# Two decoder layers on one core: the small expert's gate and up turned by transposes instead of folding matmuls

## The chip, the core and the metric

The kernel runs on one core of a Trainium2 chip, in one launch. The metric is the device time of the program in microseconds. The work of a core is split over engines that run side by side and meet at semaphores: TensorE (PE, matmuls; its weight loads are listed as PEld), VectorE (DVE), ScalarE (ACT), GpSimd (POOL), and SyncE (SP), which here issues the weight transfers.

## The reference

Two decoder layers over 256 tokens of width 1024, all in float32. Layer 0 has two kinds of sparse attention and a dense SwiGLU, layer 1 a latent attention and a mixture of 8 experts, 2 for each token. The change touches only the mixture:

```
def swiglu(h, w_gate, w_up, w_down):
    return (jax.nn.silu(h @ w_gate) * (h @ w_up)) @ w_down

    logits = (ht @ w_router).astype(jnp.float32) + b_router.astype(jnp.float32)
    top_val, top_idx = lax.top_k(logits, TOP_K)
    gates = jax.nn.softmax(top_val, axis=-1)
    combine = jnp.sum(jax.nn.one_hot(top_idx, N_EXPERTS, dtype=jnp.float32) * gates[..., None], axis=1)
    for e in range(N_EXPERTS):
        y = y + combine[:, e:e + 1].astype(h.dtype) * swiglu(ht, w_gate[e], w_up[e], w_down[e])
```

w_gate and w_up of an expert are 1024 x 3584, w_down is 3584 x 1024.

## The kernel before

**Split weights.** Each factor of a matmul is split into a high part, rounded to the PE's fast float32r, and a low part that holds the rest. Weights come in chunks of 128 x 2048 (1 MB) into `raw`, a ring of 7 slots. For each chunk SyncE issues the transfer once TensorE has used the chunk 7 before it; ScalarE writes `w_hi` (ring of 6, L665 in the mixture); VectorE writes `w_lo` (L1298) as raw minus w_hi into the place of raw; TensorE multiplies. These three steps are called the split of a chunk below.

**Pairs.** Experts are sorted by their number of tokens. A large one (up to 128 tokens) and a small one (up to 64, HALF) are run as a pair p of 84 chunks k; there are four pairs, so 336 chunks. Gate and up weights of both come in turn: 8 chunks for the large (12 matmuls of 512 columns each), 8 for the small (8 matmuls each), up to chunk 47; then 4 and 4; then 14 down chunks of the large (56 to 69) and 14 of the small (70 to 83). The hidden width 3584 is cut into 7 units j of 512, and a unit's gate and up sums are ready after the chunks that `large_ups(j)` or `small_ups(j)` names.

**A large unit.** ScalarE writes silu(gate) into `sge` (L694), VectorE multiplies it with up into `he` (L1363), TensorE turns the 128 x 512 block by four transposes (L1941), ScalarE and VectorE write the high and the low half, `e_hi` (L698) and `e_lo` (L1368).

**A small unit.** The 64 tokens stand twice in the stationary operand, on 64 partitions with their high parts and on 64 with their low parts, so that two matmuls do the work of three; gate and up then lie in PSUM as two halves over the partitions, and these have to be added. ScalarE copies gate and up into `sge` and `he` (L721, L724). TensorE turns and adds in one step: 8 fp32 matmuls (L1948) with `fold`, two identities of 64 on top of each other, into one bank. ScalarE takes the silu of the turned gate into `sT` (L716), VectorE the product into `hT` (L1387), ScalarE the high half into `es` (L727), VectorE the low half (L1391).

**Order.** Each engine runs a loop over k written out by hand. ScalarE and VectorE run 4 chunks ahead (ELEAD). `units(k, done, late)` names the units whose step falls to chunk k: `done(u) + late + u % 2 == k`. A step that stands in a loop over k waits in its place: behind it on its engine stand all splits of later chunks. Also in these loops are the gather of the next pair's tokens (L1850, at `GATHER_AT`, chunk 60), the small expert's gather (L1859), the way back to the tokens (L1877, L1878, added by VectorE at L1347), TensorE's transpose of the gated pick (L1866, at `PICK_AT`, chunk 16), and VectorE's `back` (4 chunks later), `gated_picks` (5), `picks` (8) and `small_picks` (9).

## Time and profile before

| | us |
|---|---|
| median of 3 runs | 1442.11 |
| lowest and highest | 1435.95, 1446.27 |
| the profiled execution | 1440.49 |
| its span in the profile | 1438.5 |
| TensorE busy | 1346.6 (94%) |
| VectorE busy | 1144.9 (80%) |
| ScalarE busy | 974.8 (68%) |

The mixture's chunks begin at about 514 us and end at about 1428 us of the span. The mean granted clock of TensorE over the span is 0.981 of full speed. The profile gives for each engine its busy time and, for a row, the idle time in front of it and who ended that. Matmuls are pipelined, so their busy times overlap; the distance between two starts tells what one costs.

### The profile page before, as it was taken

To read this page: it belongs to the slowest core of one execution; us is meant where nothing else is said; L and a number is where in the kernel's file an instruction comes from. 1 tells how busy PE (TensorE), PEld (TensorE's weight loads), DVE (VectorE), ACT (ScalarE), POOL (GpSimd) and SP (SyncE) were. 2 spreads that over 40 slices of the span, in tenths; PEclk is the share of its full clock that TensorE was granted. 3 is DMA by queue.
4 is the path that set the end of the run, shared out by engine and by line. 5 is a ranking of instruction groups with operands and counts; after the bars stand their busy time and mean duration, and the time that the engine had idled before them with its cause. 6 is when DMAs were issued, how large, how long until landed. Compare 5 with 4: busy or idle time off the path is not lost.

```text
span 1438.5 us, 17054 instructions
## 1 busy us (share of the span) xinstructions
PE 1346.6 (94%) x6497; PEld 1099.1 (76%) x6498; DVE 1144.9 (80%) x1161; ACT 974.8 (68%) x969; POOL 39.2 (3%) x47
## 2 busy tenths in 40 slices
PE   6987999999779889999999999999999999999996
PEld 5765788878766778778877887878877887878884
DVE  4776464462675489999899999899999999999896
ACT  4475545342477447888777878777888867788874
POOL 1012000000004000000000000000000000000000
PEclk9999999999889899999999999999999999999999
DMA  8641455553440449999999999999999999999995
GB/s 311 220 138 59 146 186 165 185 184 108 135 133 1 146 165 405 389 379 402 347 410 376 383 387 396 358 402 363 397 399 381 364 387 391 394 391 389 401 381 207
DMA packets 134940, 423.02 MB, mean 294 GB/s; under 512 B 7888, under 2 KB 14790, under 8 KB 134854
## 3 DMA queue, kind: packets, MB, share of 16 engines
q1 hardware_dynamic: 133756, 419.10, 77.8%
q0 software_dynamic: 864, 2.68, 0.6%
q8 instruction: 54, 0.88, 0.2%
q14 instruction: 32, 0.26, 0.1%
q10 hardware_dynamic: 234, 0.09, 0.0%
HBM read 420.77 MB, written 1.07 MB: 293 GB/s over the span
## 4 chain that ended last, share of the span: by engine, by line
PE 65%; DVE 20%; ACT 6%; DMA 6%; issue 3%; ACTq 0%; DVEq 0%; SPq 0%
PE PS L1510 18%; PE PS L1512 17%; PE PS L1511 17%; DVE w_lo L1298 12%; DMA raw<-in_w_up_o_dram 3%; PE PS L1948 3%; ACT w_hi L665 2%; DMA raw<-in_w_down_o_dram 2%; DVE w_lo L795 2%; PE PS L1913 1%; PE PS L1914 1%; PE PS L1850 1%; ACT w_hi L365 1%; PE PS L1859 1%; DVE he L1363 1%
## 5 line engine op out<-in xcount | busy, mean ns | idle before, releaser
L1298 DVE TENSOR_TENSOR w_lo<-raw,w_hi 128x2048 fp32r<-128x2048 f32 x336 | 762.2, 2287 | 62.1 <-ACT w_hi L665 60.0
L665 ACT ACTIVATE w_hi<-raw 128x2048 fp32r<-128x2048 f32 x336 | 639.1, 1916 | 123.5 <-DMA raw<-in_w_down_o_dram 49.4
L1510 PE MATMUL PS<-w_hi,a_hi 128*128 128x512 f32 (+5 forms) x848 | 330.1, 389 | 25.7 <-DVE w_lo L1298 14.4
L1512 PE MATMUL PS<-w_hi,a_lo 128*128 128x512 f32 (+5 forms) x848 | 323.7, 382 | 0.0
L1511 PE MATMUL PS<-w_lo,a_hi 128*128 128x512 f32 (+5 forms) x848 | 323.2, 381 | 0.0
L1510 PEld LDWEIGHTS PS<-w_hi,a_hi 128*128 128x128 f32 x848 | 161.2, 190 | 64.1 <-issue 28.9
L1512 PEld LDWEIGHTS PS<-w_hi,a_lo 128*128 128x128 f32 x848 | 161.4, 190 | 30.6
L1511 PEld LDWEIGHTS PS<-w_lo,a_hi 128*128 128x128 f32 x848 | 161.5, 190 | 27.2
L1913 PE MATMUL PS<-w_hi,a_hi 128*128 128x512 f32 x448 | 179.6, 401 | 2.2 <-DVE w_lo L1298 1.6
L1914 PE MATMUL PS<-w_lo,a_hi 128*128 128x512 f32 x448 | 175.2, 391 | 0.0
L795 DVE TENSOR_TENSOR w_lo<-raw,w_hi 128x2048 fp32r<-128x2048 f32 (+4 forms) x70 | 139.4, 2018 | 39.4 <-ACT w_hi L365 39.2
L365 ACT ACTIVATE w_hi<-raw 128x2048 fp32r<-128x2048 f32 (+4 forms) x70 | 115.4, 1698 | 12.6 <-PE PS L1512 12.6
L1913 PEld LDWEIGHTS PS<-w_hi,a_hi 128*128 128x128 f32 x448 | 84.1, 188 | 25.4 <-DVE w_lo L1298 9.2
L1914 PEld LDWEIGHTS PS<-w_lo,a_hi 128*128 128x128 f32 x448 | 84.2, 188 | 16.3
L1913 PE MATMUL PS<-w_hi,es 128*128 128x512 f32 x224 | 90.1, 402 | 5.0 <-DVE w_lo L1298 4.8
L1510 PE MATMUL PS<-w_hi,e_hi 128*128 128x512 f32 x224 | 88.9, 397 | 1.9 <-DVE w_lo L1298 1.9
L1914 PE MATMUL PS<-w_lo,es 128*128 128x512 f32 x224 | 88.3, 394 | 0.0
L1512 PE MATMUL PS<-w_hi,e_lo 128*128 128x512 f32 x224 | 88.1, 393 | 0.0
L1511 PE MATMUL PS<-w_lo,e_hi 128*128 128x512 f32 x224 | 87.8, 392 | 0.0
L1913 PEld LDWEIGHTS PS<-w_hi,es 128*128 128x128 f32 x224 | 42.1, 188 | 20.7 <-DVE w_lo L1298 6.3
L1510 PEld LDWEIGHTS PS<-w_hi,e_hi 128*128 128x128 f32 x224 | 42.1, 188 | 14.3 <-issue 4.5
L576 ACT ACTIVATE sg<-PS,nst 128x512 f32<-128x512 f32 (+1 forms) x12 | 7.2, 650 | 64.6 <-PE PS L1512 64.6
(287 smaller groups left out, 1413.5 us busy)
## 6 DMA issues: line engine op xcount, KB each, us to landing
raw<-in_w_gate_o_dram SPq DMA_DIRECT2D x112, 1024.0 KB, 9.3
raw<-in_w_up_o_dram SPq DMA_DIRECT2D x112, 1024.0 KB, 10.0
raw<-in_w_down_o_dram SPq DMA_DIRECT2D x112, 1024.0 KB, 8.0
raw<-in_w_in_e_dram SPq DMA_DIRECT2D x12, 1024.0 KB, 7.6
raw<-in_w_down_e_dram SPq DMA_DIRECT2D x11, 1024.0 KB, 4.9
raw<-in_w_gate_e_dram SPq DMA_DIRECT2D x10, 1024.0 KB, 5.1
raw<-in_w_up_e_dram SPq DMA_DIRECT2D x10, 1024.0 KB, 5.1
raw<-in_w_out_e_dram SPq DMA_DIRECT2D x4, 1024.0 KB, 5.0
```

Source lines behind the costliest of these rows:

```text
L365: nc.scalar.activation(w_hi[:, c % STG, 0:n], raw[:, c % RAW, 0:n], ACT.Copy).then_inc(hi_done, 1)
L665: nc.scalar.activation(w_hi[:, c % STG, :], raw[:, c % RAW, :], ACT.Copy).then_inc(hi_done, 1)
L795: nc.vector.tensor_tensor(w_lo[:, c % RAW, 0:n], raw[:, c % RAW, 0:n], w_hi[:, c % STG, 0:n], ALU.subtract).then_inc(lo_done, 1)
L1298: nc.vector.tensor_tensor(w_lo[:, c % RAW, :], raw[:, c % RAW, :], w_hi[:, c % STG, :], ALU.subtract).then_inc(lo_done, 1)
L1363: nc.vector.tensor_tensor(he[:, j % 2, :], PS[:, up_bank(j), :], sge[:, j % 2, :], ALU.mult)\
L1510: nc.tensor.matmul(dst, xh, wh, start=first, stop=False)
L1511: nc.tensor.matmul(dst, xh, wl, start=False, stop=False)
L1512: return nc.tensor.matmul(dst, xl, wh, start=False, stop=last)
L1850: ins = nc.tensor.matmul(PS[:, 4 + h, d * P:(d + 1) * P], xn[:, t, dc * P:(dc + 1) * P], pick[:, t, :], start=t == 0, stop=t == 1)
L1913: nc.tensor.matmul(dst, xs, wh, start=first, stop=False)
L1914: return nc.tensor.matmul(dst, xs, wl, start=False, stop=last)
L1948: ins = nc.tensor.matmul(PS[:, small_turn_bank(j), at:at + HALF], halves[:, j % 2, f * P:(f + 1) * P], fold[:, :], start=True, stop=True)
```

## The change

The 8 fp32 matmuls of a small unit's turn become 8 plain transposes. The two halves are then not added by TensorE: gate fills one whole bank and up the next, each as 4 blocks of 64 high and 64 low columns. ScalarE copies the low columns of both banks (512 elements per partition) into a new buffer `gh`; VectorE adds the high columns from PSUM to it in place; ScalarE takes the silu of the gate part in place; VectorE multiplies in place; high and low halves follow as before, each one chunk later. `SMALL_TURN` gives the first bank of a unit's two, out of the pairs 6/7, 4/5 and 2/3. To make banks 4 and 5 free, what used them there moves: transpose of the pick, back and the picks by 8 chunks, the gather by 4. `sT`, `hT` and `fold` go.

```diff
-PICK_AT, GATHER_AT = 16, DOWN_L + 4
+PICK_AT, TURN_AT, GATHER_AT = 16, 24, DOWN_L + 8
-        sT, z = place(z, "sT", [P, 2, 4 * HALF])
-        hT, z = place(z, "hT", [P, 2, 4 * HALF])
+        gh, z = place(z, "gh", [P, 2, 2, 4 * HALF])
-            return 6 + u % 2 if u < FE_TILES - 1 else 7
+        SMALL_TURN = (6, 4, 6, 4, 6, 2, 4)
...
@@ ScalarE @@
                     for j in units(k, small_ups, 5):
                         act.wait_ge(sem("sm_tr"), j + 1 + p * FE_TILES)
                         if j >= 2:
-                            act.wait_ge(sem("sm_mul"), j - 1 + p * FE_TILES)
-                        nc.scalar.activation(sT[:, j % 2, :], PS[:, small_turn_bank(j), 0:4 * HALF], ACT.Silu)\
-                            .then_inc(sem("sm_silu"), 1)
+                            act.wait_ge(sem("sm_lo"), j - 1 + p * FE_TILES)
+                        b = SMALL_TURN[j]
+                        nc.scalar.activation(gh[:, j % 2, :, :].rearrange("p u (f t) -> p u f t", f=4),
+                                             PS[:, b:b + 2, :].rearrange("p u (f h t) -> p u f h t", f=4, h=2)[:, :, :, 1, :],
+                                             ACT.Copy).then_inc(sem("sm_low"), 1)
+                    for j in units(k, small_ups, 6):
+                        act.wait_ge(sem("sm_sum"), j + 1 + p * FE_TILES)
+                        nc.scalar.activation(gh[:, j % 2, 0, :], gh[:, j % 2, 0, :], ACT.Silu).then_inc(sem("sm_silu"), 1)
...
-                    for j in units(k, small_ups, 7):
+                    for j in units(k, small_ups, 8):
                         act.wait_ge(sem("sm_mul"), j + 1 + p * FE_TILES)
                         nc.scalar.activation(es[:, 4 * j:4 * j + 4, 0:HALF],
-                                             hT[:, j % 2, :].rearrange("p (f t) -> p f t", f=4), ACT.Copy)\
+                                             gh[:, j % 2, 1, :].rearrange("p (f t) -> p f t", f=4), ACT.Copy)\
...
@@ VectorE @@
-                    for j in units(k, small_ups, 6):
+                    for j in units(k, small_ups, 5):
+                        b = SMALL_TURN[j]
+                        both = gh[:, j % 2, :, :].rearrange("p u (f t) -> p u f t", f=4)
+                        dve.wait_ge(sem("sm_low"), j + 1 + p * FE_TILES)
+                        nc.vector.tensor_tensor(both, PS[:, b:b + 2, :].rearrange("p u (f h t) -> p u f h t", f=4, h=2)[:, :, :, 0, :],
+                                                both, ALU.add).then_inc(sem("sm_sum"), 1)
+                    for j in units(k, small_ups, 7):
                         dve.wait_ge(sem("sm_silu"), j + 1 + p * FE_TILES)
-                        if j >= 2:
-                            dve.wait_ge(sem("sm_lo"), j - 1 + p * FE_TILES)
-                        nc.vector.tensor_tensor(hT[:, j % 2, :], PS[:, small_turn_bank(j), 4 * HALF:8 * HALF], sT[:, j % 2, :],
-                                                ALU.mult).then_inc(sem("sm_mul"), 1)
-                    for j in units(k, small_ups, 8):
+                        nc.vector.tensor_tensor(gh[:, j % 2, 1, :], gh[:, j % 2, 1, :], gh[:, j % 2, 0, :], ALU.mult)\
+                            .then_inc(sem("sm_mul"), 1)
+                    for j in units(k, small_ups, 9):
...
-                    if k == PICK_AT + 4:
+                    if k == TURN_AT + 4:
                         back(2 * p)
...
@@ TensorE @@
             def turn_small(j):
                 for u, halves in enumerate((sge, he)):
                     for f in range(4):
-                        at = (4 * u + f) * HALF
-                        ins = nc.tensor.matmul(PS[:, small_turn_bank(j), at:at + HALF], halves[:, j % 2, f * P:(f + 1) * P],
-                                               fold[:, :], start=True, stop=True)
+                        ins = nc.tensor.transpose(PS[:, SMALL_TURN[j] + u, f * P:(f + 1) * P], halves[:, j % 2, f * P:(f + 1) * P],
+                                                  ident)
...
-                    if k == PICK_AT:
-                        pe.wait_ge(sem("moe_add"), 8 * p + 4)
+                    if k == TURN_AT:
+                        pe.wait_ge(sem("sm_sum"), 2 + p * FE_TILES)
                         turn_pick(2 * p)
...
                     for j in units(k, small_ups, 2):
                         pe.wait_ge(sem("sm_ev"), j + 1 + p * FE_TILES)
-                        if j == FE_TILES - 1:
-                            pe.wait_ge(sem("sm_mul"), j + p * FE_TILES)
-                        else:
-                            pe.wait_ge(sem("moe_alo"), j + 1 + p * FE_TILES)
+                        if SMALL_TURN[j] == 6:
+                            pe.wait_ge(sem("moe_alo"), j + 2 + p * FE_TILES)
+                        if j == 1:
+                            pe.wait_ge(sem("moe_add"), 8 * p + 4)
+                        if j == 3:
+                            pe.wait_ge(sem("moe_back"), 2 * p + 1)
+                        if j == 5:
+                            pe.wait_ge(sem("sm_eg"), 6 + p * FE_TILES)
                         turn_small(j)
                     if follow and k == GATHER_AT:
+                        pe.wait_ge(sem("sm_sum"), FE_TILES + p * FE_TILES)
                         gather(p + 1)
```

On VectorE, in the first pair from chunk 16 on, there stands in a row before (`L1298` is the w_lo of a chunk, `x4` four chunks in a row):

```order
L1298 TENSOR_TENSOR w_lo<-raw,w_hi 128x2048 x4
L1352 TENSOR_REDUCE st<-PS 128x1
L1353 TENSOR_SCALAR backT<-PS 128x256
L1298 TENSOR_TENSOR w_lo<-raw,w_hi 128x2048
L1318 TENSOR_SCALAR pickg<-cst,pos,comb 128x128 x2
L1298 TENSOR_TENSOR w_lo<-raw,w_hi 128x2048
L1387 TENSOR_TENSOR hT<-PS,sT 128x256
L1298 TENSOR_TENSOR w_lo<-raw,w_hi 128x2048
L1387 TENSOR_TENSOR hT<-PS,sT 128x256
L1298 TENSOR_TENSOR w_lo<-raw,w_hi 128x2048
L1391 TENSOR_TENSOR es<-hT,es 128x4x64
L1304 TENSOR_SCALAR pick<-cst,pos 128x128 x2
```

And after the change, at the same place (w_lo is now L1299, the sum L1388, the product L1392, the large unit's he L1364):

```order
L1299 TENSOR_TENSOR w_lo<-raw,w_hi 128x2048 x5
L1388 TENSOR_TENSOR gh<-PS,gh 128x512
L1299 TENSOR_TENSOR w_lo<-raw,w_hi 128x2048
L1388 TENSOR_TENSOR gh<-PS,gh 128x512
L1299 TENSOR_TENSOR w_lo<-raw,w_hi 128x2048
L1392 TENSOR_TENSOR gh<-gh 128x256
L1299 TENSOR_TENSOR w_lo<-raw,w_hi 128x2048
L1392 TENSOR_TENSOR gh<-gh 128x256
L1299 TENSOR_TENSOR w_lo<-raw,w_hi 128x2048
L1396 TENSOR_TENSOR es<-gh,es 128x4x64
L1299 TENSOR_TENSOR w_lo<-raw,w_hi 128x2048
L1364 TENSOR_TENSOR he<-PS,sge 128x512
```

The back and the picks have left the place, the first sum stands one chunk ahead of where the first product stood, and the product and the halves follow one chunk later.

On ScalarE, around units 2 and 3 of the first pair, there stands before (L665 is the w_hi of a chunk, L694 the large unit's silu):

```order
L665 ACTIVATE w_hi<-raw 128x2048 x3
L716 ACTIVATE sT<-PS 128x256
L665 ACTIVATE w_hi<-raw 128x2048
L694 ACTIVATE sge<-PS 128x512
L716 ACTIVATE sT<-PS 128x256
L665 ACTIVATE w_hi<-raw 128x2048
L694 ACTIVATE sge<-PS 128x512
L727 ACTIVATE es<-hT 128x4x64
L665 ACTIVATE w_hi<-raw 128x2048
L727 ACTIVATE es<-hT 128x4x64
```

And after (w_hi is L662, the large silu L691, the copy of the low half L714, the silu L719, the high half L729):

```order
L662 ACTIVATE w_hi<-raw 128x2048 x3
L714 ACTIVATE gh<-PS 128x512
L662 ACTIVATE w_hi<-raw 128x2048
L691 ACTIVATE sge<-PS 128x512
L714 ACTIVATE gh<-PS 128x512
L719 ACTIVATE gh<-gh 128x256
L662 ACTIVATE w_hi<-raw 128x2048
L691 ACTIVATE sge<-PS 128x512
L719 ACTIVATE gh<-gh 128x256
L662 ACTIVATE w_hi<-raw 128x2048
L729 ACTIVATE es<-gh 128x4x64
```

The copy stands where sT stood, a silu for each unit has come in behind it, and the high half is one chunk later.

## Rows read from the trace of the kernel before

**Rows 1.** Windows: busy us (x rows) by engine, then clock, DMA share, GB/s.
```profile
796.30:839.10 42.80, 41.82 (x203) 33.99 (x202) 40.40 (x33) 34.59 (x28) 0.00 (x0) 1.00 1.00 387
839.10:881.30 42.20, 41.43 (x204) 34.21 (x202) 39.37 (x25) 35.56 (x28) 0.00 (x0) 1.00 1.01 381
...
796.30:1025.80 229.50, 222.85 (x1068) 182.08 (x1066) 212.71 (x138) 180.00 (x132) 0.00 (x0) 1.00 0.99 383
```

**Rows 2.** Waits from 500 to 1438 us: us in total, times, longest.
```profile
DVE w_lo L1298 <- ACT w_hi L665: 60.0, 100, 2.2
...
ACT sT L716 <- PE PS L1948: 18.0, 18, 1.8
...
ACT es L727 <- DVE hT L1387: 8.4, 8, 1.2
```

**Rows 3.** The chain of waits, 858 to 883 us: start, us on the chain.
```profile
858.23 2.20 DVE w_lo L1298
860.43 0.60 DVE he L1363
...
870.51 2.21 DVE w_lo L1298
872.86 0.47 PE PS L1510
881.29 1.75 PE PS L1948 x16
```

**Rows 4.** Timeline of PE at a large and a small unit's turn: start, us.
```profile
818.83 0.60 PE L1941 MATMUL PS<-cst,he 128*128 128x128 f32 x4
...
819.50 0.39 PE L1914 MATMUL PS<-w_lo,a_hi 128*128 128x512 f32 x1
...
843.52 1.00 PE L1948 MATMUL PS<-cst,sge 128*128 128x64 f32 x8
...
845.54 0.39 PE L1511 MATMUL PS<-w_lo,a_hi 128*128 128x512 f32 x1
```

**Rows 5.** Timeline of ACT around units 2, 3 and 4, idle before in brackets.
```profile
836.73 1.92 ACT L665 ACTIVATE w_hi<-raw 128x2048 fp32r<-128x2048 f32 x1 [0.64 <-DMA raw<-in_w_up_o_dram]
839.29 1.91 ACT L665 ACTIVATE w_hi<-raw 128x2048 fp32r<-128x2048 f32 x1 [0.64 <-DMA raw<-in_w_up_o_dram]
...
845.45 0.39 ACT L716 ACTIVATE sT<-PS 128x256 f32<-128x256 f32 x1 [1.13 <-PE PS L1948]
...
883.12 0.60 ACT L694 ACTIVATE sge<-PS 128x512 f32<-128x512 f32 x1 [2.00 <-PE PS L1948]
```

**Rows 6.** Timeline of DVE around units 2 and 3.
```profile
843.81 2.29 DVE L1298 TENSOR_TENSOR w_lo<-raw,w_hi 128x2048 fp32r<-128x2048 f32 x1 [0.28 <-ACT w_hi L665]
846.02 0.42 DVE L1387 TENSOR_TENSOR hT<-PS,sT 128x256 f32<-128x256 f32 x1
847.67 2.29 DVE L1298 TENSOR_TENSOR w_lo<-raw,w_hi 128x2048 fp32r<-128x2048 f32 x1 [1.24 <-ACT w_hi L665]
```

**Rows 7.** Groups by line and shape, 400 to 1438 us: busy us, mean ns.
```profile
L1363 DVE TENSOR_TENSOR he<-PS,sge 128x512 f32<-128x512 f32 x28 | 19.2, 684 | 0.0
...
L724 ACT ACTIVATE he<-PS 128x512 f32<-128x512 f32 x28 | 16.3, 582 | 0.2 <-PE PS L1914 0.2
...
L1391 DVE TENSOR_TENSOR es<-hT,es 128x256 fp32r<-128x256 f32 x28 | 11.7, 419 | 0.0
L1387 DVE TENSOR_TENSOR hT<-PS,sT 128x256 f32<-128x256 f32 x28 | 11.7, 417 | 0.0
L727 ACT ACTIVATE es<-hT 128x256 fp32r<-128x256 f32 x28 | 11.7, 417 | 9.2 <-DVE hT L1387 8.4
...
L716 ACT ACTIVATE sT<-PS 128x256 f32<-128x256 f32 x28 | 10.7, 382 | 18.1 <-PE PS L1948 18.0
```

**Rows 8.** Timeline of PE just after the mixture's first long wait.
```profile
516.91 0.63 PE L1511 MATMUL PS<-w_lo,a_hi 128*128 128x512 f32 x1
517.34 0.63 PE L1512 MATMUL PS<-w_hi,a_lo 128*128 128x512 f32 x1
```

More of the change, by code:

```diff
@@ L212, in hybrid_trunk @@
         backT, z = place(z, "backT", [P, S], f32r)
-        fold = cst[:, K_MASK:K_MASK + HALF]
         PS = ctx.enter_context(nc.psum_tensor("PS", [P, 8, NT], f32))
@@ L256, in small_up_bank @@
             return u % 2 if u < FE_TILES - 1 else 1
-        def small_turn_bank(u):
-            return 6 + u % 2 if u < FE_TILES - 1 else 7
+        SMALL_TURN = (6, 4, 6, 4, 6, 2, 4)
         def pair_chunk(k):
@@ L1279, in by_size @@
                 step(ins)
-                step(nc.vector.tensor_tensor(fold[:, :], ident[:, 0:HALF], ident[:, HALF:P], ALU.add))
             def combine():
@@ L1390, in pair @@
+                    for j in units(k, small_ups, 7):
+                        dve.wait_ge(sem("sm_silu"), j + 1 + p * FE_TILES)
+                        nc.vector.tensor_tensor(gh[:, j % 2, 1, :], gh[:, j % 2, 1, :], gh[:, j % 2, 0, :], ALU.mult)\
+                            .then_inc(sem("sm_mul"), 1)
+                    for j in units(k, small_ups, 9):
                         dve.wait_ge(sem("sm_hi"), j + 1 + p * FE_TILES)
                         nc.vector.tensor_tensor(es[:, 4 * j:4 * j + 4, HALF:P],
-                                                hT[:, j % 2, :].rearrange("p (f t) -> p f t", f=4),
+                                                gh[:, j % 2, 1, :].rearrange("p (f t) -> p f t", f=4),
@@ L1393, in pair @@
                                                 es[:, 4 * j:4 * j + 4, 0:HALF], ALU.subtract).then_inc(sem("sm_lo"), 1)
-                    if k == PICK_AT + 4:
+                    if k == TURN_AT + 4:
                         back(2 * p)
-                    if k == PICK_AT + 5:
+                    if k == TURN_AT + 5:
                         gated_picks(p + PAIRS, p + PAIRS, HALF)
-                    if follow and k == PICK_AT + 8:
+                    if follow and k == TURN_AT + 8:
                         picks(p + 1, P)
-                    if follow and k == PICK_AT + 9:
+                    if follow and k == TURN_AT + 9:
@@ L1968, in pair_waits @@
                     else:
-                        pe.wait_ge(sem("moe_back"), 2 * p + 1)
+                        pe.wait_ge(sem("sm_sum"), 4 + p * FE_TILES)
                 elif kl == DOWN:
@@ L1973, in pair_waits @@
                     else:
-                        pe.wait_ge(sem("sm_eg"), FE_TILES - 1 + units0)
+                        pe.wait_ge(sem("sm_sum"), FE_TILES - 1 + units0)
                 if kl >= DOWN and (kl - DOWN) % 2 == 0:
@@ L1995, in pair @@
                         if j >= 2:
-                            pe.wait_ge(sem("sm_mul"), j - 1 + p * FE_TILES)
+                            pe.wait_ge(sem("sm_sum"), 2 * (j // 2) - 1 + p * FE_TILES)
                         else:
@@ L2001, in pair @@
                         pe.wait_ge(sem("sm_ev"), j + 1 + p * FE_TILES)
-                        if j == FE_TILES - 1:
-                            pe.wait_ge(sem("sm_mul"), j + p * FE_TILES)
-                        else:
-                            pe.wait_ge(sem("moe_alo"), j + 1 + p * FE_TILES)
+                        if SMALL_TURN[j] == 6:
[6 more added lines that the diff above has]
+                            pe.wait_ge(sem("sm_eg"), 6 + p * FE_TILES)
                         turn_small(j)
                     if follow and k == GATHER_AT:
+                        pe.wait_ge(sem("sm_sum"), FE_TILES + p * FE_TILES)
                         gather(p + 1)
                     if k == DOWN_S + 3:
-                        pe.wait_ge(sem("sm_mul"), FE_TILES + p * FE_TILES)
+                        pe.wait_ge(sem("sm_sum"), FE_TILES + p * FE_TILES)
                         if follow:
```

## The prediction

> **What bounds the kernel now.** I read the windows first, then the waits, the chain and the timelines. Everything the change touches lies in the mixture of experts, four pairs of 84 chunks of 1 MB, some 229 us a pair. Over one pair TensorE is busy 222.9 of 229.5 us, VectorE 212.7, ScalarE 180.0, and the transfers show a share of 0.99 of their 16 engines [rows 1]. So three resources stand within 8% of each other: taking work from one of them hits the next soon. The reader should see in the waits that VectorE waits 60.0 us for ScalarE's w_hi, that ScalarE waits 18.0 us for the small expert's turn (L1948) at its sT, and that it waits 8.4 us in 8 places for VectorE's product [rows 2]. The chain shows where each engine sets the time: VectorE row by row in the small expert's chunks (858.23 to 870.51, with 0.60 us for each 512-wide row between two w_lo of 2.20 us), then TensorE from 872.86 through the large expert's chunks and the turn at 881.29 [rows 3]. TensorE thus paces the large phases, with the turns in them; VectorE and the transfers pace the small ones. In the steady stretch the splits of ScalarE start 2.56 us apart (836.73, 839.29) because transfers land so [rows 5]. 16 chunks at that pace are 41.0 us, and the window of 16 chunks takes 42.2 [rows 1]: no more than 1.2 us is to be had in such a group before the transfers are the bound. The group before it, read from turn to turn in the same way, takes 42.8, so 1.8.
>
> **The turn on TensorE.** A small unit's turn now runs from 843.52 to the point from which the next matmuls run at full pace: the second of them starts at 845.54, matmuls of 512 columns start 0.23 apart, so the turn costs 845.54 - 0.23 - 843.52 = 1.79 us for 16 passes (8 fp32 matmuls, two records each). The large unit's four transposes run from 818.83 in the same way to 819.50 - 0.23, which is 0.44 us; their 0.60 us of busy time with 0.27 for the last makes 0.11 us from one to the next [rows 4]. Eight transposes are then 0.44 + 4 x 0.11 = 0.88 us, and a turn loses 0.91 us. 28 turns: 25.5 us of TensorE.
>
> **VectorE.** Before, a unit has a product of 256 (L1387, PSUM source, 417 ns) and a low half of 256 (L1391, 419 ns). After, it has a sum of 512 with one PSUM operand, the shape of L1363 (684 ns busy, 0.60 in the chain), a product of 256 from SBUF like L1391, and the same low half [rows 3, 7]. Busy times overlap the next row by 0.08, so 256 elements cost 0.34 on the path. Added: 0.60 us a unit, 16.8 us in all. No row reads PSUM in runs of 64; I take the contiguous row's price, between nothing extra and twice it, and take the row because its element count and engines are the same. The Trainium skill, Perfetto Trace Analysis, in its tips on VectorE and ScalarE, puts an instruction's data access at some 60 ns from SBUF and 125 ns from PSUM for VectorE; by that the product from SBUF would be 65 ns cheaper, 1.8 us over 28 units. Rows L1387 and L1391 differ by 2 ns the other way, so the trace does not bear it out here.
>
> **ScalarE.** sT (382 ns from PSUM) becomes a copy of 512 out of PSUM, like L724 (582 ns), and a Silu of 256 from SBUF, like L727 (417 ns) [rows 7]: about 0.6 us a unit, 17 us in all, beside 180 of 229.5 us busy. It has room for it, except where someone waits for the split behind it.
>
> **What of this lies on the path, place by place.** I step through one pair.
> *Units 0 to 3 (two groups of 16 chunks).* At 845.45 ScalarE's sT of the second unit has waited 1.13 us for TensorE, the split behind it comes late, and VectorE, done with its row at 846.02, idles 1.24 us until 847.67 [rows 5, 6]. After the change both turns before that point are shorter, 1.8 us together, so the copy of the low half starts when ScalarE is free, and that stall goes. In its place come two sums, 1.20 us. The first falls into the slack that VectorE has while it runs at the transfers' 2.56 against its own 2.21 (0.35 us a chunk). Net for VectorE: -1.24 + 1.20 - 0.35, some -0.4 us. That is the floor. The ceiling is the transfers' pace, 1.2 to 1.8 us, 1.5 on average. It is approached because a slot of raw is refilled only when TensorE has used it: chunks finished up to 1.8 us sooner refill the ring sooner. I take the middle, 0.9 us a group, 1.8 a pair.
> *Units 4 and 5.* At 883.12 ScalarE's sge has waited 2.00 us for the turn at 881.29 [rows 3, 5], so the shorter turn counts directly, -0.91. From there to the split of the first down chunk VectorE sets the pace; that stretch had two products (0.68) and now has two sums and one product (1.54): +0.86. Net nothing (-1.2 to +0.5).
> *Unit 6.* Its turn lies among 14 large chunks in a row, where TensorE is the bound: -0.91, the sum beside it. At worst the following small chunks swallow it.
> *What only moves.* back, the gated picks and both picks (some 1.9 us a pair on VectorE) go 8 chunks later, TensorE's transpose of the pick from chunk 16 to 24, the gather from chunk 60 to 64. The first four leave the place where the two sums now stand, and land before the next large phase. Queued behind them are w_lo rows that TensorE reaches only later in that phase; without that cover they cost what they free at the old place. I cost both at nothing. The new waits on TensorE (for sums) name sums that VectorE issues before the w_lo that TensorE has already used, so they are met. ScalarE's Silu waits for a sum of the chunk before; behind it is queued the next split, and VectorE waits for that. The fold constant goes (one row). SP's and POOL's queues keep their order.
>
> Sum per pair: 1.8 + 0 + 0.9 = 2.7 us; four pairs 10.9 us. The profiled execution took 1440.5 us (span 1438.5), the median is 1442.1, so the first becomes 1429.6 and the second **1431**. Bounds of the unknowns: 0.4 x 2 - 0.5 + 0 = 0.3 us a pair gives 1441; 1.5 x 2 + 1.2 + 0.9 = 5.1 us a pair gives 1422. A change under 1%, 14.4 us, can hardly be told from none in this kernel.
>
> **Rivals.**
> *The sums eat it.* VectorE is 93% busy and takes 16.8 us more; if the refill of the ring gains nothing, only the floor is left: 1441. For it: 858.23 to 870.51 has no gap on VectorE [rows 3]. Against: TensorE's share is higher still. Chance 0.20.
> *More than forecast.* If TensorE's lag is what starves the transfers everywhere, also in the down chunks and after the gathers, 25.5 us of it come back nearly in full and each pair goes towards 84 x 2.56 = 215 us until VectorE's 217 bounds it. 5 to 6 us a pair: 1420. For it: 14.5 us a pair lie between 229.5 and 215. Against: VectorE would have to be 97% busy. Chance 0.20.
> *Slower, by the handshake.* A unit now passes between ScalarE and VectorE six times instead of four: low half, sum, Silu, product, high, low. The sum stands in the same chunk as the copy it needs. If the copy ends more than VectorE's 2.2 us after the split before it, VectorE stands still with all its w_lo behind it, and TensorE behind those. A wait of this kind (es for the product) costs 8.4 / 8 = 1.05 us [rows 2]. If every unit pays half of it beside its own sum, 28 x (0.5 + 0.6) = 31 us stand against what the places above save before their sums, 2 x (1.24 + 0.35) + 2 x 0.91 = 5.0 us a pair, 20 us: 1453. It decides where TensorE is over 1.6 us behind at the copy; sT waited 1.0 us on average (18 times), before turns got shorter. Chance 0.12.
> *It doesn't do what it says.* If an fp32 transpose took two passes like the fold, no turn would get shorter and the sums would remain: 16.8 us less the slack of 0.35 at 8 of them, so 1456. Rows L1941 show one record each, 0.11 apart [rows 4]. Chance 0.02.
> *The clock.* Around both kinds of turn the granted clock is 1.00, the upper level of 2.4 GHz [rows 1]; where it was low, after waits of TensorE, 512 columns start 0.43 apart instead of 0.23 [rows 8]. If the 8 transposes let it fall for one large chunk of 12 matmuls, that costs 2.4 us; at the 16 places where turns follow each other, 38 us: 1469. The Trainium skill, TensorE: Matmul & The Clock Gate, in its part on the PE-mode transpose, says that transposes don't count as activity for the clock, which speaks against this change. The large unit's four transposes leave the matmuls behind them at 0.23, so here the trace disagrees, for four. Chance 0.02.
>
> **How the numbers follow.** Forecast 0.44, with a range of its own from 1422 to 1441; the rest as above. The range reaches from the case of more gain to past the case of none, 1417 to 1447, which leaves out the three slow rivals (0.16) and a little below. Faster by over 1% (under 1427.7): 0.20 and a third of the forecast, 0.35. Within 1%: the rest of the forecast and the case where the sums eat it, 0.49. Slower: 0.16.
>
> **What the profile after would show.** Turns of 0.9 us with no matmul slowed behind them; ScalarE's waits for the turn at the copy a few us in all instead of 18; VectorE over 95% busy in a pair and its waits for w_hi down from 60 to some 35 us; a sum of 0.68 busy; ScalarE waiting for VectorE at Silu and at es; pairs of some 226.5 us. I am wrong if VectorE waits for the low half, if the sum's runs of 64 cost more than 0.7 us, or if the transfers pace the kernel more than the windows tell.

## The result

| us | before | after |
|---|---|---|
| median of 15 runs each | 1442.11 | **1431.52** |
| lowest and highest | 1435.95, 1446.27 | 1427.64, 1436.51 |
| profiled execution: span | 1438.5 | 1429.7 |

The ratio is 0.9932, with a 95% interval from 0.9917 to 0.9947: a gain of 0.7%, 10.6 us by the medians, beside the 1431 that were forecast. What of the working was right, and what came out even by errors against each other, has to be read by place.

The changed kernel's page, first its span, then busy time, share and instructions by engine:

```profile
span 1429.7 us, 16640 instructions
...
PE 1328.3 (93%) x6273; PEld 1071.7 (75%) x6274; DVE 1158.4 (81%) x1188; ACT 985.8 (69%) x997; POOL 39.1 (3%) x47
```

TensorE has lost 18.3 us of busy time and VectorE has gained 13.5 (1144.9 before). The windows of the second pair, as in [rows 1], show the whole pair and its first two stretches, cut at the turns of units 0, 2 and 4 (busy us and rows by engine, clock, DMA share, GB/s):

```profile
791.30:1018.00 226.70, 217.86 (x1009) 175.16 (x1008) 216.89 (x145) 183.19 (x138) 0.00 (x0) 1.00 1.00 390
791.30:834.60 43.30, 41.01 (x188) 32.33 (x187) 43.03 (x35) 38.14 (x31) 0.00 (x0) 1.00 1.03 409
834.60:875.90 41.30, 40.22 (x186) 32.12 (x185) 39.95 (x27) 34.57 (x30) 0.00 (x0) 1.00 1.02 384
...
```

The reader should see that TensorE and VectorE now stand within 1 us of each other in a pair (217.86 and 216.89 of 226.70), and that VectorE fills the first stretch to 43.03 of 43.30.

The waits from 500 to 1430 us (total, times, longest), which answer to [rows 2]:

```profile
DVE w_lo L1299 <- ACT w_hi L662: 35.6, 66, 2.0
...
ACT gh L719 <- DVE gh L1388: 12.2, 12, 1.7
...
ACT gh L714 <- PE PS L1952: 8.7, 12, 1.2
...
ACT es L729 <- DVE gh L1392: 6.5, 12, 0.9
```

VectorE's wait for w_hi fell from 60.0 to 35.6 us, ScalarE's for the turn from 18.0 to 8.7, and a new one of 12.2 us stands at the Silu, for VectorE's sum. The turn itself, in PE's timeline, which answers to [rows 4]:

```profile
1021.66 0.60 PE L1952 MATMUL PS<-cst,sge 128*128 128x128 f32 x4
1022.10 0.60 PE L1952 MATMUL PS<-cst,he 128*128 128x128 f32 x4
1022.46 0.48 PE L1515 MATMUL PS<-w_hi,a_hi 128*128 128x512 f32 x1
1022.77 0.40 PE L1516 MATMUL PS<-w_lo,a_hi 128*128 128x512 f32 x1
```

1022.77 - 0.23 - 1021.66 = 0.88 us, and the matmuls behind it start 0.23 apart (the third stands at 1023.00).

The most useful reading is the distance from one turn's start to another's, because the turns stand at the same chunks in both kernels. Means over the four pairs (three for the last stretch), in us:

| | 0 to 2 | 2 to 4 | 4 to 6 | 6 to next 0 | first turn to end |
|---|---|---|---|---|---|
| before | 42.68 | 42.41 | 23.30 | 121.00 | 872.3 |
| after | 42.88 | 41.28 | 23.11 | 119.42 | 864.6 |
| forecast for after | 41.8 | 41.5 | 23.3 | 120.1 | |

(The forecast row is before less 0.9, 0.9, 0 and 0.9.) The last column is span less start of the first turn: 1438.5 - 566.25 and 1429.7 - 565.12. It leaves out the head of the program, which is nearly the same code in all kernels here but whose length differs from one profiled execution to another by up to 10 us (first turns from 559.0 to 568.8), and so it compares the mixtures more closely than the spans do.

The gain is not where it was put: nothing in the first stretch, more than forecast in the last.

### The profile page after: what moved, and what is told of

The parts are those of the page before. It is cut to its first block, busy times and chain, and to the rows that moved or that the text cites. A ratio compares the mean times of both kernels' runs of the same rounds, so it can differ in the third digit from the quotient of the medians.

```text
span 1429.7 us, 16640 instructions
## 1 busy us (share of the span) xinstructions
PE 1328.3 (93%) x6273; PEld 1071.7 (75%) x6274; DVE 1158.4 (81%) x1188; ACT 985.8 (69%) x997; POOL 39.1 (3%) x47
## 4 chain that ended last, share of the span: by engine, by line
PE 63%; DVE 25%; ACT 5%; DMA 5%; issue 2%; ACTq 0%; DVEq 0%; SPq 0%
PE PS L1515 17%; PE PS L1517 16%; PE PS L1516 16%; DVE w_lo L1299 16%; DMA raw<-in_w_down_o_dram 2%; PE PS L1918 2%; PE PS L1919 2%; DMA raw<-in_w_up_o_dram 2%; ACT w_hi L662 2%; DVE w_lo L797 2%; PE PS L1952 1%; PE PS L1855 1%; ACT w_hi L362 1%; PE PS L1864 1%; DVE he L1364 1%
## 5 line engine op out<-in xcount | busy, mean ns | idle before, releaser
L1299 DVE TENSOR_TENSOR w_lo<-raw,w_hi 128x2048 fp32r<-128x2048 f32 x336 | 761.7, 2285 | 37.7 <-ACT w_hi L662 35.6
L662 ACT ACTIVATE w_hi<-raw 128x2048 fp32r<-128x2048 f32 x336 | 638.0, 1914 | 102.3 <-DMA raw<-in_w_down_o_dram 38.7
L1918 PE MATMUL PS<-w_hi,a_hi 128*128 128x512 f32 x448 | 182.0, 406 | 11.5 <-DVE w_lo L1299 10.6
```

Of the source, the lines that this page charges most:

```text
L662: nc.scalar.activation(w_hi[:, c % STG, :], raw[:, c % RAW, :], ACT.Copy).then_inc(hi_done, 1)
L1299: nc.vector.tensor_tensor(w_lo[:, c % RAW, :], raw[:, c % RAW, :], w_hi[:, c % STG, :], ALU.subtract).then_inc(lo_done, 1)
L1918: nc.tensor.matmul(dst, xs, wh, start=first, stop=False)
```

## The experiments

Ratios are to the kernel before in the same batch, with 95% intervals. Differences between two kernels of different batches carry both intervals. For the distances there is one profiled execution of each kernel.

**1. The turn alone.**

```diff
-  ins = nc.tensor.matmul(PS[:, small_turn_bank(j), at:at + HALF], halves[:, j % 2, f * P:(f + 1) * P],
-                         fold[:, :], start=True, stop=True)
+  ins = nc.tensor.transpose(PS[:, small_turn_bank(j), at:at + HALF],
+                            halves[0:HALF, j % 2, f * P:(f + 1) * P], ident[0:HALF, 0:HALF])
```

> The kernel before, with only the turn made short: 8 transposes of 64 partitions in place of the 8 folding matmuls. Left out: the low halves are not added, so the small expert's units miss them; nothing is added on VectorE or ScalarE and no step moves. Theory of the prediction (the turn's 1.79 us lie on the path, the sums give a part back): the two groups of 16 chunks gain up to the transfers' pace, 1.2 to 1.8 us each, the turn of unit 4 and that of unit 6 0.9 each, some 4.5 us a pair, 1424 us (ratio 0.987). Rival, the gain comes from the moved steps (the gather and the picks) and not from the turn: within 3 us of before, 1440.

Measured: 1423.14 us, ratio 0.9875 [0.9852, 0.9898]; stretches 41.37, 41.04, 22.02, 119.58, and 852.3 us from the first turn to the end. All four stretches shrink by 1.3 to 1.4 us. PE's timeline at the turn:

```profile
828.68 0.46 PE L1948 MATMUL PS<-cst,sge 64*128 64x64 f32 x4
828.98 0.41 PE L1948 MATMUL PS<-cst,he 64*128 64x64 f32 x4
...
829.66 0.39 PE L1511 MATMUL PS<-w_lo,a_hi 128*128 128x512 f32 x1
```

829.66 - 0.23 - 828.68 = 0.75 us: from 64 rows instead of 128 this turn is 0.13 us shorter than the changed kernel's, 3.6 us over 28 turns, so this kernel is a little better than "the turn alone" should be. Experiment 12 was made for that reason.

**2. The moves alone**, in the kernel before: back, picks and the transpose of the pick 8 chunks later, the gather 4.

```diff
-PICK_AT, GATHER_AT = 16, DOWN_L + 4
+PICK_AT, TURN_AT, GATHER_AT = 16, 24, DOWN_L + 8
...
```

> The kernel before, with only the steps moved: transpose of the pick, back, gated picks and picks 8 chunks later, the gather 4 chunks later; the folding turn stays. Prediction: these moves cost nothing, within 2 us of before (1440 to 1444). Rival, read from the intervals between the turns of both traces, where the stretch from unit 6 to the next pair's unit 0 got 2.1 to 2.5 us shorter in two of three pairs: the later gather gives that, so 3 x 2 us faster, 1436.

Measured: 1440.57 us, 1.000 [0.9978, 1.0022]; stretches 43.57, 42.35, 23.29, 120.57. With the old turns the medians don't tell the moves from free, give or take 3 us; the one profiled execution is 3.0 us longer from the first turn to the end (875.2). The first stretch grows by 0.9 us and the last is 0.4 shorter.

**3. Each turn made twice**, in the changed kernel, so that a turn takes again what it took before.

```diff
-                for u, halves in enumerate((sge, he)):
+                for u, halves in 2 * list(enumerate((sge, he))):
```

> The changed kernel with each turn's 8 transposes issued twice (16 passes, about 1.76 us, as long as the folding turn was). All sums and moves stay. Theory that TensorE's turn lies on the path: the gain of the turn goes and the sums' cost remains, 1431.5 + 13 to 20 = 1445 to 1452 us, slower than the kernel before. Rival, VectorE is the bound now and hides TensorE's extra time: within 4 us of the changed kernel, 1435 at most.

Measured: 1449.89 us, 1.006 [1.0036, 1.0083]; 44.41, 42.95, 23.99, 120.08. Against the changed kernel that is 0.0128 more, 18 us for 28 x 0.88 = 24.6 us of TensorE's time. Three quarters of a turn lie on the path. ScalarE's waits for the turn at the copy rise from 8.7 to 25.1 us:

```profile
ACT gh L714 <- PE PS L1952: 25.1, 18, 2.3
```

**4. VectorE's sum made twice.** A second row of 448 elements (the same blocks, 56 columns of each) goes ahead of each sum, into room that nobody reads.

```diff
                         dve.wait_ge(sem("sm_low"), j + 1 + p * FE_TILES)
+                        spare = cst[:, K_MASK:K_LOW].rearrange("p (u f t) -> p u f t", u=2, f=4)
+                        if j + p:
+                            dve.wait_ge(sem("sm_spare"), j + p * FE_TILES)
+                        nc.vector.tensor_tensor(spare, PS[:, b:b + 2, :].rearrange("p u (f h t) -> p u f h t", f=4, h=2)[:, :, :, 0, 0:56],
+                                                cst[:, 0:448].rearrange("p (u f t) -> p u f t", u=2, f=4), ALU.add)\
+                            .then_inc(sem("sm_spare"), 1)
```

> The changed kernel with a second row on VectorE ahead of each sum: 448 elements from the same banks and a constant, written to a place that nobody reads. By the price of the 512-wide row that is 0.53 us each, 28 of them, 14.8 us of VectorE. If VectorE is the bound throughout the mixture: + 15 us, 1446. If it is so only in the group of units 0 to 3, as its timeline shows (no idle from the first sum on for 35 us): half of it, 1439. If transfers or TensorE set the pace there: within 3 us of 1431.5.

Measured: 1439.64 us, 0.9997 [0.9974, 1.0019]; 43.82, 41.48, 24.17, 119.76. 0.0065 more than the changed kernel, 9 us (give or take 4) for some 14.8 us of VectorE's time. It stands in the first (+0.9) and the third stretch (+1.1), where VectorE was full; in the second and the last, +0.2 and +0.3.

**5. The picks still later**, behind the next large phase.

```diff
-                    if k == TURN_AT + 5:
+                    if k == TURN_AT + 20:
                         gated_picks(p + PAIRS, p + PAIRS, HALF)
-                    if follow and k == TURN_AT + 8:
+                    if follow and k == TURN_AT + 21:
                         picks(p + 1, P)
-                    if follow and k == TURN_AT + 9:
+                    if follow and k == TURN_AT + 22:
                         small_picks(p + 1)
```

> The changed kernel with gated picks and both picks another 15 and 13 chunks later (chunks 44 to 46), out of the stretch from unit 0's turn to unit 2's and into the next, where the trace of the turn alone shows the transfers' pace (41.0 us for 16 chunks) and VectorE has 0.35 us a chunk to spare. Theory, VectorE sets the first stretch (42.9 us, no idle): that stretch gets 0.7 to 1.2 us shorter, the next keeps its 41.3, 3 to 4 us in all, ratio to before 0.9905. Rival, that stretch is set by TensorE or by the transfers, its length has nothing to do with the picks: as the changed kernel, 0.993.

Measured: 1432.93 us, 0.9939 [0.9913, 0.9964]; 42.12, 42.26, 23.11, 119.10. The first stretch gives up 0.76 us and the second takes 0.98. The second stretch doesn't keep its 41.3 us, as it was expected to: the work is paid wherever it stands in these two stretches.

**6 to 8. Work taken off VectorE.** Experiment 6 puts the product of gate and up on GpSimd, 7 the low half as well, 8 is 6 with the late picks of 5.

```diff
-                    for j in units(k, small_ups, 7):
-                        dve.wait_ge(sem("sm_silu"), j + 1 + p * FE_TILES)
-                        nc.vector.tensor_tensor(gh[:, j % 2, 1, :], gh[:, j % 2, 1, :], gh[:, j % 2, 0, :], ALU.mult)\
-                            .then_inc(sem("sm_mul"), 1)
...
+            for p in range(PAIRS):
+                for j in range(FE_TILES):
+                    pool.wait_ge(sem("sm_silu"), j + 1 + p * FE_TILES)
+                    nc.gpsimd.tensor_tensor(gh[:, j % 2, 1, :], gh[:, j % 2, 1, :], gh[:, j % 2, 0, :], ALU.mult)\
+                        .then_inc(sem("sm_mul"), 1)
```

> The changed kernel with the in-place product of gate and up on GpSimd, which can take it now that both stand in SBUF; VectorE loses 28 rows of 0.34 us, 9.5 us. Theory, VectorE bounds units 0 to 3's first stretch and the one from unit 4 to 6: 0.7 and 0.3 us less there, some 4 us in all, ratio 0.990. Rival 1, the transfers bound the rest and VectorE nothing: 0.993. Rival 2, GpSimd's access to SBUF slows VectorE's rows (w_lo over 2.29 us) or its product comes too late for ScalarE's es: slower than the changed kernel, 0.995 or more.

> As e6, with the low half es on GpSimd too: VectorE loses 28 more rows of 0.34 us, 19 us in all. By the theory the two stretches come within 0.3 us of those of the turn alone, 0.988 to 0.989. If GpSimd disturbs VectorE, worse than e6.

> e5 and e6 together. The theory adds them where both shorten the first stretch, down to the transfers' 41.0 us: 0.988 to 0.989. If VectorE was not the bound there: 0.993.

Measured: 1431.42 us, 0.9937 [0.9913, 0.9961]; 1433.64, 0.9949 [0.9927, 0.9971]; 1431.56, 0.9947 [0.9925, 0.9968]. None can be told from the changed kernel, so what the theory promised (0.988 to 0.990) came in none. The stretches are 42.65, 41.00, 23.29, 119.41 in 6; 43.26, 41.44, 23.29, 119.40 in 7; 42.29, 42.06, 23.28, 119.47 in 8. The groups by shape (busy us, mean ns of one) show where the relief went. Of experiment 6:

```profile
L1299 DVE TENSOR_TENSOR w_lo<-raw,w_hi 128x2048 fp32r<-128x2048 f32 x336 | 764.3, 2298 | 41.2 <-ACT w_hi L662 39.4
...
L1509 POOL TENSOR_TENSOR gh<-gh 128x256 f32<-128x256 f32 x28 | 55.3, 1976 | 805.8 <-ACT gh L719 805.8
```

Of experiment 7:

```profile
L1299 DVE TENSOR_TENSOR w_lo<-raw,w_hi 128x2048 fp32r<-128x2048 f32 x336 | 776.2, 2338 | 41.9 <-ACT w_hi L662 40.1
```

The w_lo rows of VectorE were busy for 761.7 us in the changed kernel, 764.3 in 6 and 776.2 in 7; by the mean of one (2285, 2298 and 2338 ns), 336 rows take 4.4 us more in 6 and 17.8 in 7. Two rows of 0.34 us for 28 units are 19 us off VectorE's path in 7, and nearly all of it comes back. In 6 9.5 us are saved and 4.4 come back, but these stand in 16 single rows, each beside a product on GpSimd: 0.16 us more at units 1 and 3, 0.37 at units 5 and 6. The row beside the product of unit 5, in the third pair of experiment 6:

```profile
L1299 DVE TENSOR_TENSOR w_lo<-raw,w_hi x1: 2654/2654/2654, 1116.1 to 1116.1; 128x2048 fp32r<-128x2048 f32 x1
```

That row lies on the chain of waits between the turns of units 4 and 6 (2.67 us there, beside 2.21 in the changed kernel). The product's 0.34 us leave that chain and the longer row fills the place, so the third stretch is not shorter but 0.18 us longer. (The split that waits behind the Silu comes onto the chain as well then, less than 0.1 us after VectorE could have started.)

**9 to 11. The Silu and all behind it one chunk later**, so that ScalarE no longer stands at the sum (9); with the product on GpSimd (10); with the late picks too (11).

```diff
-                    for j in units(k, small_ups, 6):
+                    for j in units(k, small_ups, 7):
                         act.wait_ge(sem("sm_sum"), j + 1 + p * FE_TILES)
```

(and product, high and low half from 7, 8 and 9 to 8, 9 and 10)

> The changed kernel with Silu, product, high and low half each one chunk later, so that ScalarE's Silu no longer waits for a sum of the chunk before (12.2 us of such waits, 1.13 at unit 5 with the split of the next chunk behind it). Theory that this wait is what holds the stretch from unit 4's turn to unit 6's at 23.1 us (22.0 with the turn alone): it gets 0.3 to 1.0 us shorter, VectorE's own rows keep the rest; 1 to 4 us in all, ratio to before 0.990 to 0.992. Rival, VectorE's rows hold it: no change, 0.993 to 0.994.

> e9 with the product on GpSimd as in e6. In e6 the product's absence from VectorE changed nothing in the stretch from unit 4 to 6 because the Silu's wait came last. If so, both together bring it to 22.3 or less and the first stretch to 42 or less: ratio 0.988 to 0.990. If the two don't add, 0.993.

> e10 with the picks late as in e5, the version with all three, a candidate that beats both kernels. If VectorE still has too much over the two stretches together, as e5 shows (one got 0.8 us shorter, the next 1.0 longer), the picks' place stays without effect: as e10. If e10 has freed the first two stretches down to the transfers' 41 us each, 0.987.

Measured: 1432.29 us, 0.9937 [0.9914, 0.996]; 1432.17, 0.9946 [0.9924, 0.9967]; 1435.54, 0.9963 [0.9944, 0.9982]. The stretches are 43.43, 41.20, 22.74, 119.74 in 9; 43.15, 41.27, 23.28, 119.32 in 10; 42.44, 42.30, 23.29, 120.20 in 11. In 9 the wait at the Silu goes and the third stretch is 22.74 instead of 23.11, but the first is 43.43 instead of 42.88, and ScalarE's waits for the product at es rise from 6.5 to 12.0 us. The chain of waits shows that it was not the Silu's wait that gave the 0.37 us. Between the turns of units 4 and 6 the changed kernel's chain runs over VectorE alone from 1105.99 on, up to TensorE's next matmul. Its last rows in the third pair are:

```profile
1111.69 0.60 DVE gh L1388
1112.29 2.20 DVE w_lo L1299
1114.48 0.34 DVE gh L1392
1114.82 2.21 DVE w_lo L1299
```

In 9 the product (L1392) stands one chunk later, and the chain ends without it:

```profile
1110.59 0.60 DVE gh L1388
1111.19 4.41 DVE w_lo L1299 x2
```

In 10 the product runs on GpSimd beside the second of these rows. The two take 0.54 us more and the gain is gone; the third stretch had been expected at 22.3 us or less:

```profile
1115.91 4.95 DVE w_lo L1299 x2
```

Experiment 11, built to beat both kernels, is 0.0031 slower than the changed one, some 4 us, give or take 3; its profiled execution, from which the stretches are, was its slowest. In 10 and 11 ScalarE waits at es for GpSimd's product, by up to 4.1 and 4.8 us at a time.

**12. The changed kernel without its sums.** ScalarE copies the high columns, and whoever waited for a sum waits for that copy.

```diff
-                    for j in units(k, small_ups, 5):
-                        b = SMALL_TURN[j]
-                        both = gh[:, j % 2, :, :].rearrange("p u (f t) -> p u f t", f=4)
-                        dve.wait_ge(sem("sm_low"), j + 1 + p * FE_TILES)
-                        nc.vector.tensor_tensor(both, PS[:, b:b + 2, :].rearrange("p u (f h t) -> p u f h t", f=4, h=2)[:, :, :, 0, :],
-                                                both, ALU.add).then_inc(sem("sm_sum"), 1)
...
-                        act.wait_ge(sem("sm_sum"), j + 1 + p * FE_TILES)
+                        act.wait_ge(sem("sm_low"), j + 1 + p * FE_TILES)
...
```

> The changed kernel without VectorE's sums: ScalarE copies the high columns and everything that waited for a sum waits for that copy, so the low halves are left out of gate and up. Turns, moves, the copy of 512 and the later steps stay as changed. It prices the sum inside the changed kernel, with its own turn of 0.88 us; the turn alone (e1_turn_only) had a shorter one, 0.75 us, from 64 rows instead of 128. If VectorE's time is worth 60% on the path, as the second sum showed (+9 us for 14.8), 16.8 us of sums cost 10 us: 0.9932 - 0.007 = 0.986. If the sums cost only what lies between the changed kernel and the turn alone after its shorter turns are paid for (8.2 less 0.75 x 3.6 = 5.5 us): 0.989. If the new order (copy, Silu and halves one chunk later, moves) is what costs, and the sum is hidden: 0.992 or more. In the first stretch of a pair, which VectorE bounds, the distance from turn 0 to turn 2 should fall from 42.9 to about 41.7 us; unit 6's stretch should change by less than 0.4.

Measured: 1427.29 us, 0.9916 [0.9893, 0.994]; stretches 42.97, 41.17, 21.98, 119.34, and 858.9 us from the first turn to the end. This went against the expectation by VectorE's time (0.986): the ratio is nearest the third case (0.992 or more), in which the sum is hidden, and the first stretch does not fall to 41.7. VectorE's timeline at its start, in the third pair, shows why, with the idle time in brackets:

```profile
1012.40 2.29 DVE L1299 TENSOR_TENSOR w_lo<-raw,w_hi 128x2048 fp32r<-128x2048 f32 x1 [0.26 <-ACT w_hi L662]
1014.97 2.29 DVE L1299 TENSOR_TENSOR w_lo<-raw,w_hi 128x2048 fp32r<-128x2048 f32 x1 [0.28 <-ACT w_hi L662]
1018.05 2.30 DVE L1299 TENSOR_TENSOR w_lo<-raw,w_hi 128x2048 fp32r<-128x2048 f32 x1 [0.79 <-ACT w_hi L662]
1020.26 0.42 DVE L1386 TENSOR_TENSOR gh<-gh 128x256 f32<-128x256 f32 x1
...
1033.87 0.41 DVE L1353 TENSOR_REDUCE st<-PS 128x1 f32<-128x256 f32 x1
...
```

It idles 0.26, 0.28 and 0.79 us ahead of three rows, has no gap from 1018.05 to 1059, and in that full part come the back (1033.87) and the picks. In experiment 1, with turns a little shorter still and the back and picks at their old place, VectorE does them where it otherwise idles. In its second pair, shown here, it runs on without a gap from 786.40 to 829, and its first stretch is 1.6 us shorter on average:

```profile
786.40 2.29 DVE L1298 TENSOR_TENSOR w_lo<-raw,w_hi 128x2048 fp32r<-128x2048 f32 x1 [0.27 <-ACT w_hi L665]
788.61 0.42 DVE L1352 TENSOR_REDUCE st<-PS 128x1 f32<-128x256 f32 x1
788.95 0.42 DVE L1353 TENSOR_SCALAR backT<-PS 128x256 fp32r<-128x256 f32 x1
```

**The account.** From the first turn to the end of the span:

| | us | step |
|---|---|---|
| before | 872.3 | |
| turn alone (1) | 852.3 | -20.0 |
| with turns of 0.88 us, the copy of 512, the Silu apart, new buffers, order and moves, no sums (12) | 858.9 | +6.6 |
| with the sums (after) | 864.6 | +5.7 |

The second step is 1.60 us a pair in the first stretch, 6.4 in all, and the other stretches change by at most 0.24. It holds the moves and much besides, and no run takes it apart further. The third is 1.13 us in the third stretch, 4.5 in all, and nothing in the first (42.97 and 42.88). The medians of all runs agree but are coarser: 1 to 12 is 0.0041, some 6 us, give or take 5; 12 to after is 0.0016, some 2 us, give or take 4. By medians alone the sum is not told from free; that it costs some 5 us rests on one profile of each and on the place where the difference stands.

## Why the prediction was right, and where it was not

**The turn: right.** 0.88 us forecast and measured (0.87 and 0.89 in the chain), 16 passes to 8. Experiment 3 puts 24.6 us of turns back for 18 us. Experiment 1 takes 28 x (1.79 - 0.75) = 29.1 us out, for 20 by the profile and 18 by the medians. So 0.73 of the turns' time lay on the path in 3, and 0.62 to 0.69 in 1.

**The sum's price: right.** The profile's groups, which answer to [rows 7]:

```profile
L1364 DVE TENSOR_TENSOR he<-PS,sge 128x512 f32<-128x512 f32 x28 | 19.1, 682 | 0.0
L1388 DVE TENSOR_TENSOR gh<-PS,gh 128x512 f32<-128x512 f32 x28 | 19.1, 681 | 0.0
...
L714 ACT ACTIVATE gh<-PS 128x512 f32<-128x512 f32 x28 | 16.6, 593 | 8.7 <-PE PS L1952 8.7
...
L719 ACT ACTIVATE gh<-gh 128x256 f32<-128x256 f32 x28 | 11.7, 418 | 12.2 <-DVE gh L1388 12.2
L1392 DVE TENSOR_TENSOR gh<-gh 128x256 f32<-128x256 f32 x28 | 11.7, 418 | 0.0
```

The sum takes 681 ns beside 682 of the contiguous L1364: runs of 64 columns cost nothing extra. The product from SBUF takes 418 ns where the one from PSUM took 417 [rows 7], so the trace shows no difference. The Trainium skill, Perfetto Trace Analysis, in its section Optimizing Scalar/DVE Operations, puts VectorE's access at some 60 ns from SBUF and 125 ns from PSUM; the 65 ns less that one would estimate from it did not come here.

**Units 0 to 3: the second stretch right, the first wrong.** Forecast were -0.9 and -0.9 us. The second group gave -1.13 and stands at 41.28, near the 40.96 that 16 chunks take at the transfers' 2.56; experiment 1 reaches 41.04 there. The first gave +0.20. What failed is **"I cost both at nothing"** of what only moves. With long turns (experiment 2) the first stretch already grew by 0.9 us. With short turns the step that holds the moves costs 1.6 us there. The cover named ("w_lo rows that TensorE reaches only later") was not there. The old place was one where VectorE had slack at the transfers' pace, the new one lies in its full part (experiment 12). In the changed kernel's chain of the third pair the back, the gated picks and the picks are on the path, 1.57 us together, and the rows behind them end in TensorE's first matmul at 1055.38:

```profile
1041.55 0.33 DVE st L1353
1041.88 0.33 DVE backT L1354
...
1044.41 0.52 DVE pickg L1319 x2
...
1052.73 0.39 DVE pick L1305 x2
1053.12 2.21 DVE w_lo L1299
1055.38 0.51 PE PS L1515
```

The chain of experiment 1 in the same stretch of its third pair has VectorE's rows for the large unit and no back, gated picks or picks between them:

```profile
1028.15 0.68 DVE he L1363
...
1031.64 8.80 DVE w_lo L1298 x4
1040.44 0.60 DVE e_lo L1368
1041.04 2.21 DVE w_lo L1298
```

(In its second pair the chain runs over VectorE through the whole stretch and has them in it; 41.95 us beside the changed kernel's 43.26.) That the 1.60 us are the moves' rests on these chains and on experiments 2 and 5. It is not shown by a run of its own, and up to 0.26 us of it can be the two turns, each 0.13 us longer than experiment 1's.

The sums, on the other hand, which the forecast charged to this place, are hidden there: they fall into the 0.28 and 0.79 us which VectorE idles without them (experiment 12). The changed kernel's timeline, which answers to [rows 6]:

```profile
1020.01 2.29 DVE L1299 TENSOR_TENSOR w_lo<-raw,w_hi 128x2048 fp32r<-128x2048 f32 x1 [0.26 <-ACT w_hi L662]
1022.22 0.69 DVE L1388 TENSOR_TENSOR gh<-PS,gh 128x512 f32<-128x512 f32 x1
1022.82 2.28 DVE L1299 TENSOR_TENSOR w_lo<-raw,w_hi 128x2048 fp32r<-128x2048 f32 x1
1025.02 0.68 DVE L1388 TENSOR_TENSOR gh<-PS,gh 128x512 f32<-128x512 f32 x1
1025.66 2.29 DVE L1299 TENSOR_TENSOR w_lo<-raw,w_hi 128x2048 fp32r<-128x2048 f32 x1
```

**Units 4 and 5: right, with its reason.** Forecast 0, measured -0.19 (23.30 to 23.11). The shorter turn counts there in full and more (22.02 in experiment 1, -1.28), and the sums take it back (+1.13 between 12 and after; forecast +0.86 for sums and products). The chain has what the forecast counted: two sums and one product, in place of two products. ScalarE's timeline, which answers to [rows 5], shows the waits at the Silu beside it:

```profile
1108.13 0.60 ACT L714 ACTIVATE gh<-PS 128x512 f32<-128x512 f32 x1
1108.92 0.42 ACT L719 ACTIVATE gh<-gh 128x256 f32<-128x256 f32 x1 [0.19 <-DVE gh L1388]
...
1112.32 0.42 ACT L719 ACTIVATE gh<-gh 128x256 f32<-128x256 f32 x1 [1.13 <-DVE gh L1388]
```

In the changed kernel these waits cost nothing: the chain shown under experiments 9 to 11 runs over VectorE, which has no gap from 1105.99 to past 1117, and when the wait went (9), the 0.37 us gained were those of the product that left the chain (0.34).

**Unit 6 and the down chunks: mis-sized.** Forecast -0.9, measured -1.58 on average, but -2.5, -2.1 and -0.2 in the three pairs; -1.42 in experiment 1, -1.66 in 12. The sum beside it is free, as forecast (119.34 us without it, 119.42 with it). That more than the turn's 0.91 comes is seen in all three kernels; it is not explained, and the spread between pairs is as large as the excess. The moves alone (experiment 2) shorten this stretch by 0.43 us, no more than that spread. The head (-1.1 us) and the tail (+1.5) take part in the difference of the two spans and are no more than the spread of the profiled executions.

So the sum of 10.9 us came out at 8.8 in the profiled executions' spans and 10.6 in the medians. By place: four times 1.1 us less than forecast in the first stretch, against four times 0.2 more in each of the next two and three times 0.7 more in the last; behind the fourth pair's last turn, where the forecast had its fourth 0.9 us, the tail is 1.5 us longer instead, and the head 1.1 us shorter. From the first turn to the end the profile shows a gain of 7.7 us. That the median came within 1 us of the forecast is therefore luck in part: the working is borne out in its mechanisms and to some 3 us, not to 1.

**The rivals.** *The sums eat it*: they take back 5.7 us of 20 by the profiles, not all. *More than forecast*: experiment 1 shows that the mechanism is real (1.3 to 1.4 us in every stretch), and that in the changed kernel the moves and the sums stand against it. *The handshake*: the waits are there (12.2 us at the Silu, 6.5 at es), but VectorE never stood still for a low half, and at units 4 and 5, where the Silu's wait is longest, it is not on the chain; the point from which it decides, a late copy at every unit, was not reached since waits for the turn fell to 8.7 us. *It doesn't do what it says* and *the clock* fall by the PE timeline: 8 records 0.11 apart, matmuls 0.23 apart behind them, the granted clock at 1.00 in all windows of the pair (the upper level, 2.4 GHz). The rule of the Trainium skill, TensorE: Matmul & The Clock Gate, in Part 4 on the PE-mode transpose, that transposes don't count as activity for the clock, changes nothing here with eight in a row, and nothing with sixteen in experiment 3, where the matmuls behind a turn start 0.23 us apart too and the granted clock is 1.00.

**The signs to look for** were right in their numbers: VectorE's wait for w_hi 35.6 us (some 35), 95.7% of a pair (over 95%), pairs of 226.2, 226.7 and 227.7 us (226.5), the sum at 0.68 busy.

Not tried: the back and picks at their old place in the changed kernel, which would be the direct test of how much of the 1.6 us is theirs. Their banks 4 and 5 are taken there by the turn of unit 1, so it needs another plan of the banks. No version beat the changed kernel; the kernels that gave less time leave the sums out.

## What to carry to other kernels

Where two engines and the transfers are within a few per cent, ask of a step that moves not what is queued behind it but whether the engine has slack at the old place and at the new one: here 1.9 us of small rows were moved by 8 chunks out of the slack, and the step that holds them ate a third of what shorter turns had won. Measure distances between the same instruction in both kernels, stretch by stretch; totals that agree with a forecast can hide two errors of opposite sign. Before work is moved to an idle engine, look at whether rows on the busy one get longer beside it, and look at the rows beside it and not at a mean over all. A wait that goes together with a gain need not be its cause: compare the chains of both kernels.

## What the runs showed of the hardware

- Rows on GpSimd lengthen VectorE's rows: w_lo means 2285 ns alone, 2298 with one 128x256 product a unit on GpSimd, 2338 with two rows a unit. A single row beside one product took up to 2656 ns (experiment 6), beside two rows up to 2833 (experiment 7). A 128x256 float32 product took 1976 ns on GpSimd by the profile, which is rough for that engine, and 418 on VectorE.
- PSUM read in blocks of 64 columns, every other block, cost VectorE the same as contiguous columns (681 and 682 ns), and ScalarE nearly so (593 and 582 ns for 512 elements).
- An fp32 transpose leaves one record and takes 0.11 us in a row of them, 128x128; with 64 rows to 64 columns four take 0.30 us instead of 0.44.
